# Mixture-of-experts blocks: the down projection in three rounded products, with its weights split once per block

## The reference

```python
xb = x2d[tok]                                          # 128 x 1024
hb = jax.nn.silu(xb @ exp_w1[e]) * (xb @ exp_w3[e])    # 128 x 256
return hb @ exp_w2[e]                                  # 128 x 1024, the down projection
```

## Time and profile before

| | |
|---|---|
| median of 3 runs | 2145.06 us (2141.28 to 2153.23) |
| profiled execution, its own time | 2144.8 us |
| its span in the profile | 2143.0 us |
| mean granted TensorE clock | 0.963 |
| TensorE busy over the span | 1948.6 us (91%) |
| TensorE weight loads | 1320.2 us (62%) |
| VectorE busy | 1225.0 us (57%) |
| ScalarE busy | 1027.3 us (48%) |
| GpSimd busy | 746.7 us (35%) |
| bytes moved | 380.62 MB, mean 178 GB/s |

### The profile page before, as it was taken

The page is one execution under the profiler, slowest core; times in us unless marked ns, Lnnn a source line. Parts: engine busy times, 40 slices in busy tenths (PEclk is TensorE's granted clock), DMA queues, the critical chain, the costliest instruction groups (busy, mean ns, idle before and its releaser), DMA issues. The chain is left out here.

```text
span 2143.0 us, 31045 instructions
## 1 busy us (share of the span) xinstructions
PE 1948.6 (91%) x8581; PEld 1320.2 (62%) x8582; DVE 1225.0 (57%) x1818; ACT 1027.3 (48%) x1478; POOL 746.7 (35%) x764
## 2 busy tenths in 40 slices
PE   4787998999998899599999999999999999999980
PEld 2344444558898455366776776767777777666760
DVE  2376445200678579785566566556656656555556
ACT  3354542100224211265666666666666666665652
POOL 4211000000004114444656544346656663335340
PEclk8899999999999899699999999999999999999995
DMA  8742100110103322535975998975688788987854
GB/s 258 236 140 99 58 20 20 49 39 17 15 1 122 110 89 89 196 127 199 290 274 137 318 339 255 305 213 150 193 258 249 240 269 286 301 284 254 284 141 179
DMA packets 108984, 380.62 MB, mean 178 GB/s; under 512 B 28413, under 2 KB 42749, under 8 KB 83965
## 3 DMA queue, kind: packets, MB, share of 16 engines
q1 hardware_dynamic: 62508, 261.05, 32.9%
q0 software_dynamic: 46128, 118.81, 21.8%
q10 hardware_dynamic: 290, 0.02, 0.0%
HBM read 336.59 MB, written 81.45 MB: 195 GB/s over the span
## 5 line engine op out<-in xcount | busy, mean ns | idle before, releaser
L1961 DVE TENSOR_TENSOR wupl<-big,wuph 128x2048 fp32r<-128x2048 f32 x234 | 525.9, 2289 | 453.4 <-ACT wuph L1899 449.3
L1899 ACT ACTIVATE wuph<-big 128x2048 fp32r (+1 forms) x234 | 435.9, 1916 | 8.5 <-SPq L1639 5.0
L1824 PE MATMUL bank<-w,hT 128*128 (+1 forms) x920 | 414.1, 593 | 0.5 <-issue 0.5
L1803 PE MATMUL bank<-wuph,xTh 128*128 128x512 f32 x928 | 371.7, 401 | 6.5 <-DVE xTl L1970 6.3
L1803 PE MATMUL bank<-wuph,xTl 128*128 128x512 f32 x928 | 364.5, 393 | 0.0
L1803 PE MATMUL bank<-wupl,xTh 128*128 128x512 f32 x928 | 363.3, 392 | 0.0
L1737 POOL DMA_INDIRECT yacc_scratch<-y,idx_s x106 | 208.8, 1969 | 411.7 <-issue 369.7
L1824 PEld LDWEIGHTS bank<-w,hT 128*128 128x128 f32 x920 | 166.0, 190 | 166.0 <-issue 165.9
L1889 ACT ACTIVATE y<-bank 128x512 f32<-128x512 f32 x115 | 68.8, 598 | 286.0 <-PE bank L1824 246.0
L1803 PEld LDWEIGHTS bank<-wuph,xTh 128*128 128x128 f32 x928 | 175.7, 189 | 42.1 <-issue 8.5
L1803 PEld LDWEIGHTS bank<-wuph,xTl 128*128 128x128 f32 x928 | 174.4, 188 | 37.0
(11 more groups left out here) (347 smaller groups left out, 2494.0 us busy)
## 6 DMA issues: line engine op xcount, KB each, us to landing
big<-in_exp_w SPq DMA_DIRECT2D x128, 1024.0 KB, 9.1
w<-in_exp_w SPq DMA_DIRECT2D x64, 1024.0 KB, 8.7
wada<-in_w_ada POOLq DMA_DIRECT2D x16, 1024.0 KB, 6.5
wada<-in_w_ada SPq DMA_DIRECT2D x4, 2048.0 KB, 12.2
wg<-in_w_in SPq DMA_DIRECT2D x8, 1024.0 KB, 5.6
x<-x_scratch SPq DMA_DIRECT2D x9, 512.0 KB, 4.1
x_scratch<-x SPq DMA_DIRECT2D x9, 512.0 KB, 3.6
hn_scratch<-hn SPq DMA_DIRECT2D x9, 512.0 KB, 2.9
```

The source lines that it names most:

```text
L1803: mm = pe.matmul(b_up[j][:, :], x[:, k, :], w[:, :, k, :], start=(k == 0 and i == 0), stop=(k == KT - 1 and i == 2))
L1824: mm = pe.matmul(b_down[half][:, :], hT[:, i, :], w2[:, at, i, half * 512:(half + 1) * 512].rearrange("p s n -> p (s n)"), start=(i == 0), ...
L1899: act.activation(part13(wup[j][0], half), raw13(e % WSLOT, half), ACT.Copy).then_inc(w_high, 1)
L1961: dve.tensor_tensor(part13(wup[j][1], half), raw13(e % WSLOT, half), part13(wup[j][0], half).bitcast(F32), ALU.subtract).then_inc(w_low, 1)
```

## The change

The hidden rows and the down weights are now split in high and low too, and `down` issues twelve float32r matmuls of 512 columns in place of four float32 ones. The weights' split is made anew for every block, into one pair of buffers (`wdn`), and `hT` is a pair as well. ScalarE's and VectorE's orders are new:

- ScalarE: `high(b+2)` first half, `y_half(b-1)`, `down_part(b)` (copy of 2048 columns of w2), `ht(b)`, `high(b+2)` second half, `silu(b+1)`, `xt(b+2)`. The result of the last block is copied after the loop.
- VectorE: `low(b+2)` first half, `down_rest(b)` (subtraction of 2048, both inputs in SBUF), `h_rest(b)` (subtraction of 256 with one input in PSUM), `low(b+2)` second half, `hidden(b+1)`, `x_low(b+2)`.
- TensorE no longer reads the expert's number nor waits for w2; `issue_down` waits for the splits of the slot's last block (`down_low`) in place of its down projection. `hs` and `hb` move into an unused end of a big buffer.

```diff
+        hT = [sb(f"hT5{part}", [P, 2, P], F32R) for part in "hl"]
+        wdn = [sb(f"wdn{part}", [P, 2, D], F32R) for part in "hl"]
...
-                sp.wait_ge(down_done, ends(e - WSLOT, r))
+                sp.wait_ge(down_low, 2 * ends(e - WSLOT, r))
...
-                pe.wait_ge(w2_ready, e + 1)
-                pe.wait_ge(ht_ready, b + 1)
+            def down(b):
+                pe.wait_ge(down_high, 2 * b + 2)
+                pe.wait_ge(down_low, 2 * b + 2)
                 pe.wait_ge(y_act, b + 1)
+                (hh, hl), (wh, wl) = hT, wdn
                 for half in range(2):
+                    c = slice(half * 512, (half + 1) * 512)
                     for i in range(2):
-                        mm = pe.matmul(b_down[half][:, :], hT[:, i, :],
-                                       w2[:, at, i, half * 512:(half + 1) * 512].rearrange("p s n -> p (s n)"),
-                                       start=(i == 0), stop=(i == 1))
+                        for n, (h, w) in enumerate(((hh, wh), (hh, wl), (hl, wh))):
+                            mm = pe.matmul(b_down[half][:, :], h[:, i, :], w[:, i, c], start=(i == 0 and n == 0), stop=(i == 1 and n == 2))
                 mm.then_inc(down_done, 1)
...
+            def down_part(b, q=None):
+
+                e = 0 if q is None else expert(act, q)
+                act.wait_ge(w2_ready, e + 1)
+                if not (isinstance(b, int) and b == 0):
+                    act.wait_ge(down_done, b)
+                act.activation(wdn[0][:, :, :].rearrange("p i n -> p (i n)"), raw2(e % WSLOT), ACT.Copy).then_inc(down_high, 1)
...
             with act.Fori(0, n) as r:
                 for u in range(2):
                     b, j = r * 2 + (u + NSH), (u + NSH) % 2
+                    high(r * 2 + (u + NSH + 2), j, 0, r * 2 + (u + 2))
+                    y_half(r * 2 + (u + NSH - 1), 1 - j)
+                    down_part(b, r * 2 + u)
                     ht(b)
-                    high(r * 2 + (u + NSH + 2), j, r * 2 + (u + 2))
+                    high(r * 2 + (u + NSH + 2), j, 1, r * 2 + (u + 2))
                     silu(r * 2 + (u + NSH + 1), 1 - j)
                     xt(r * 2 + (u + NSH + 2), j)
-                    y_half(b, j)
+            y_half(n * 2 + (NSH - 1), (NSH - 1) % 2)
...
+            def down_rest(b, q=None):
+
+                e = 0 if q is None else expert(dve, q)
+                dve.wait_ge(w2_ready, e + 1)
+                if not (isinstance(b, int) and b == 0):
+                    dve.wait_ge(down_done, b)
+                dve.wait_ge(down_high, 2 * b + 1)
+                dve.tensor_tensor(wdn[1][:, :, :].rearrange("p i n -> p (i n)"), raw2(e % WSLOT),
+                                  wdn[0][:, :, :].rearrange("p i n -> p (i n)").bitcast(F32), ALU.subtract).then_inc(down_low, 1)
+
+            def h_rest(b):
+
+                dve.wait_ge(down_high, 2 * b + 2)
+                dve.tensor_tensor(hT[1][:, :, :], b_h[:, 0:DE].rearrange("p (i n) -> p i n", i=2),
+                                  hT[0][:, :, :].bitcast(F32), ALU.subtract).then_inc(down_low, 1)
...
                 for u in range(2):
                     j = (u + NSH) % 2
-                    low(k * 2 + (u + NSH + 2), j, k * 2 + (u + 2))
+                    low(k * 2 + (u + NSH + 2), j, 0, k * 2 + (u + 2))
+                    down_rest(k * 2 + (u + NSH), k * 2 + u)
+                    h_rest(k * 2 + (u + NSH))
+                    low(k * 2 + (u + NSH + 2), j, 1, k * 2 + (u + 2))
                     hidden(k * 2 + (u + NSH + 1), 1 - j, k * 2 + (u + 1))
                     x_low(k * 2 + (u + NSH + 2), j)
```

More of the change, by code:

```diff
@@ L1553, in stage_experts @@
         idx_g, idx_s = ([sb(f"idx_{n}{j}", [P, 1], I32) for j in range(2)] for n in "gs")
-        hs, hb = [sb(f"hs{j}", [P, DE]) for j in range(2)], [sb(f"hb{j}", [P, DE]) for j in range(2)]
-        hT = sb("hT5", [P, 2, P])
+        hs, hb = ([m.tail[:, (2 * i + j) * DE:(2 * i + j + 1) * DE] for j in range(2)] for i in range(2))
+        hT = [sb(f"hT5{part}", [P, 2, P], F32R) for part in "hl"]
+        wdn = [sb(f"wdn{part}", [P, 2, D], F32R) for part in "hl"]
         y = [sb(f"y{j}", [P, D]) for j in range(2)]
@@ L1851, in _ @@
                 turn(b + 2, b % 2)
-                down(b, b % 2)
+                down(b)
                 if b == 1:
@@ L1864, in _ @@
                     turn(r * 2 + (u + NSH + 2), j)
-                    down(b, j, r * 2 + u)
+                    down(b)
         @block.scalar
@@ L1890, in y_half, with high @@
                 act.activation(y[j][:, 512:1024], b_down[1][:, :], ACT.Copy).then_inc(y_act, 1)
-            def high(b, j, q=None):
+            def high(b, j, part, q=None):
                 e = 0 if q is None else expert(act, q)
[L1895 to L1899, removed]
+                if part == 0:
+                    act.wait_ge(w_ready, e + 1)
+                    if not (isinstance(b, int) and b < 2):
+                        act.wait_ge(up_done, b - 1)
+                half = HALVES[part]
+                act.activation(part13(wup[j][0], half), raw13(e % WSLOT, half), ACT.Copy).then_inc(w_high, 1)
             def places_out():
@@ L1913, in _ @@
             act.sem_inc(y_act, 1)
-            high(0, 0)
+            for part in range(2):
+                high(0, 0, part)
             xt(0, 0)
             xt(1, 1)
-            high(1, 1)
+            for part in range(2):
+                high(1, 1, part)
             silu(0, 0)
             for b in range(NSH):
+                ahead = b + 2 - NSH if b + 2 >= NSH else None
+                high(b + 2, b % 2, 0, ahead)
+                if b >= 1:
+                    y_half(b - 1, (b - 1) % 2)
+                down_part(b)
                 ht(b)
-                high(b + 2, b % 2, b + 2 - NSH if b + 2 >= NSH else None)
+                high(b + 2, b % 2, 1, ahead)
                 silu(b + 1, (b + 1) % 2)
                 xt(b + 2, b % 2)
-                y_half(b, b % 2)
                 if b == 1:
@@ L2014, in _ @@
             slots(NT - 2)
-            low(0, 0)
+            for part in range(2):
+                low(0, 0, part)
             x_low(0, 0)
             x_low(1, 1)
-            low(1, 1)
+            for part in range(2):
+                low(1, 1, part)
             hidden(0, 0)
@@ L2022, in _ @@
                     dve.wait_ge(tail_act, TAB)
-                low(b + 2, b % 2, b + 2 - NSH if b + 2 >= NSH else None)
+                ahead = b + 2 - NSH if b + 2 >= NSH else None
+                low(b + 2, b % 2, 0, ahead)
+                down_rest(b)
+                h_rest(b)
+                low(b + 2, b % 2, 1, ahead)
                 if b + 1 == NSH:
```

37 lines of the change are left out of this document (18 added, 19 removed).

## The result

The changed kernel takes 2156.03 us (median of 20 runs, 2152.27 to 2162.78), the one before 2145.91 in its 20 runs beside it (2140.72 to 2154.29). The ratio is 1.0041, 95% interval 1.003 to 1.0053: some 10 us slower, just under the 0.5% named in the prediction. The forecast was 21 us faster, and the time lies just outside the range (2156.03 against an upper end of 2156). The profiled execution's span is 2153.6 us against 2143.0.

A forecast was written before the change was run, and what follows sets the result against it. It took TensorE's order to bound the loop now, and the chain through the split afterwards. 48 us gained, less 16 for 38 blocks without gain, less 11 for slower scatters, gave 21: 2124 us, range 2094 to 2156.

The forecast's parts named there:

- TensorE's share: Down projection: 3.44 us removed, twelve float32r matmuls 0.229 us apart added, 2.74 us; period falls 0.70 to 9.35 us.
- The chain sets the end, not TensorE: Expert loop: y, weight split, hidden and x_low delay the up matmuls; 9.63 us a block, 0.42 less, 48 us over 115.
- The 14 + 18 blocks, and some six more ... gain nothing: 77 blocks are left: Blocks already at the scatters' pace gain nothing; 77 x 0.42 = 32 us remains of 48.
- two stretches: 1252.81 to 1404.75 and 1759.28 to 1953.24: scatters claimed slower than blocks, 10.85 and 10.78 us each.
- calm stretches: Loop blocks where scatters do not set the pace: period of 9.6 us expected, scatter slack about 0.4 us.
- the rival: Scatters become the clock everywhere: VectorE delays GpSimd, intervals grow 0.6 to 0.8 us, 2155 to 2165 us; chance 0.2.
- Scatters slower by VectorE, 11 us: GpSimd held out by VectorE's subtractions: 0.3 us more per scatter, 38 x 0.3 = 11 us in scatter-set stretches.

The follow-up runs named there:

- b_two: The kernel before, with scatters going in turn to two accumulators in HBM so two can be in flight; 2157.7 us, ratio 1.0069.
- b_zero: b_two with the second accumulator zeroed in an earlier stage and the shared blocks storing once; 2159.31 us, ratio 1.0049.
- a_places: The changed kernel with TensorE's table work issued ahead of the down projection in shared blocks 1 and 3; 2151.57 us, ratio 1.0024.
- a_nosplit: The changed kernel with the down weights split only at block 0 and that split used by all later blocks; 2149.1 us, ratio 1.0012.
- a_ylate: The changed kernel, one accumulator, with the copy of y behind down_part instead of in front; 2182.19 us, ratio 1.0171.
- a_two: The changed kernel with TensorE's table work first and scatters going in turn to two accumulators in HBM; 2130.36 us, ratio 0.9944.
- a_best: a_two with zeroed second accumulator, single stores, earlier free-buffer message for block 4, three tiles added by VectorE; 2126.1 us, ratio 0.9923.

## Why the prediction was wrong, point by point

**TensorE's share: right.** The down matmuls stand 0.23 apart (1506.43 to 1506.66).

**The chain sets the end, not TensorE: right, a size off.** The predicted order of links, the wait of the up matmuls for `x_low` and the alternation of late and early blocks are all there. Predicted 9.63, measured 9.73 with the scatters away. 106 blocks at 0.32 are the 33.9 us that the pair without scatters shows; the prediction had 0.42. The 0.10 would fit two things that I see in the rows but did not test: `down_part` starts after 0.36 us of "issue" (the register read, costed at nothing and bounded at 0.26), and y starts up to 0.3 late behind the `high` in front of it.

**"The 14 + 18 blocks, and some six more ... gain nothing: 77 blocks are left": this is the step that failed.** It saw the scatters as a clock in two stretches and gave the other 77 blocks the whole gain, 32 us, as if there the scatters had any room asked for. The loop gained 0. The calm stretches did have room (21 scatters waited for their rows), but its size was never set against the gain. Scatters one by one took 9.75 us in the kernel before: beside TensorE's 10.05 that is 0.3 us of room, and the planned 9.63 is already beyond it. On top of that the landings came 0.32 us later in the changed kernel (8.96 against 8.64), which makes it 10.07. What the scatters cost the loop went from 10.6 us to 44.6. That this ate the gain to the last 0.1 us is chance. That the wait for a single scatter takes the gain is shown by both pairs without it (33.9 us of loop without scatters, 33.0 with two in flight); why the landings are later is open.

The reading of the two stretches was off as well, though it mattered less. The scatters went at 10.8 there, the blocks mostly not: the y copies of the first stretch are 10.05 us apart until 1380, those between 1759 and 1953 on the mean 10.37, and the whole loop lost 10.6 us to the scatters. The row cited for the rival, 10.30 us for 68 intervals "no less than the blocks' own 10.05", can't carry it either: a mean interval of the scatters follows that of the blocks, whichever of the two sets the pace.

**Scatters slower by VectorE, 11 us: the size is seen, the cause is not.** The scatters are longer on GpSimd by 0.28 us (the predicted 0.3), and they land 0.32 us later, in all of the loop and not in 38 blocks. But GpSimd's time is not what their interval is made of: it is 10.17 at 1.99 us a scatter and 10.15 at 2.25, and b_two's scatters, with 1.61 of GpSimd, take 8.63 to land against 8.64 in the kernel before with 1.97. The rule of the Trainium skill, "SBUF — State Buffer", Who interferes with whom, fits its first half again (3.73 us for the first scatter of the loop, issued 0.08 us into a subtraction, 1.60 for the last); subtractions of 2048 stay at 2286 ns on the mean, none over 2.33 us, so the other half is not seen here either. No run shows that rule's 0.28 us in the pace of the scatters.

**The shared blocks: not in the sum.** The prediction followed one block of the loop and gave all 115 its gain. In the nine shared ones VectorE also makes the lists and tables, some 16 us in three groups, and TensorE's table work follows `down`. There the chain through VectorE meets them, and 11.5 us go. That it is the weights' split is shown (87.4 without it, 98.2 with). That TensorE's order carries some 3 us of it rests on one profile (95.0) and a median lower by 4.5 us. That the rest is VectorE's groups is argued from the rows above; no run takes them away.

**The rivals.** Slower was given 0.2, by way of the scatters. It was right that in the changed kernel they would hold the whole loop (102 of 106 wait for a landing), and near in the room that it gave the calm stretches (0.4 us; 0.3 by the rows above). It was wrong in the price: it wanted intervals 0.15 us longer, and it looked for the trouble in VectorE alone, not in the shorter loop itself. The mean interval stayed at 10.15, the gain went to 0, and the loss came from the shared blocks. So the kernel was slower, but not by this rival's way.

In numbers: predicted 48 - 16 - 11 = 21 us faster; measured 0 in the loop and 11.5 lost in the shared blocks, 10.6 of span.

## What to carry to other kernels

Before pricing a shorter loop, take each serial resource in it (here one accumulating scatter in flight) and work out how long one use takes by itself: from issue to landing, plus the step from a landing to the next issue where nothing else is waited for. Here that is 8.64 + 1.11 = 9.75 us. Set it against the period that you plan and not against the present one; if it isn't clearly below, the loop ends where the resource does, and earlier still when single uses vary as these do. Its mean interval (last less first, over the count) won't tell, because buffers tie it to the loop's whichever is slower. To learn what such a wait costs, take it away in both kernels: the gain appears at once, 33 us in the loop and 25 in all between the two kernels with two accumulators. And price the written-out blocks ahead of a loop by themselves, since engines that are half idle in the loop may not be so there.

## What was not expected of the hardware

An indirect DMA that adds 128 rows of 4 KB takes 8.7 us from issue to landing at the median in the kernel before (4.4 to 12.8) with GpSimd busy for only 1.6 to 2.3 of them; waited for one by one, that is 10.15 us a scatter, whether the engine's part is 1.99 or 2.25 us. Two in flight take 9.1 to 9.9 us each at the median, and the loop no longer feels them, at the same DMA share of 0.8. The mean time to landing goes with the order of the loop and not with the number in flight: 8.6 to 8.7 us in the three kernels of the old order (before, b_two, b_zero), 8.9 to 9.1 in five of the new (after, a_places, a_nosplit, a_ylate, a_two), one execution each; nothing here says why. Filling the second accumulator and adding it in the end is not free: from the last y copy to the end it is 59 us with one, 73 with two and double stores, 77 with two and zeros (72 in a_best).
